# Output products in two halves of K, the first behind the last scores

## What is computed

```python
# first block: sliding-window heads (columns 0:512), differential heads (512:1024)
x = x + jnp.concatenate([out_a, out_b], axis=-1) @ w_out[l]
x = x + cross_attention(rms_norm(x, g_cross[l]), rms_norm(mem, g_mem[l]), w_cq[l], w_ckv[l], w_co[l])
x = x + jnp.square(jax.nn.relu(rms_norm(x, g_mlp[l]) @ w_up[l])) @ w_down[l]
# second block, two layers (mod = silu(c) @ ada_w + ada_b gives shifts, scales, gates)
x = x + 0.5 * g1[:, None] * swiglu(h, ff_w13[l, 0], ff_w2[l, 0])
y = hybrid_conv_mla(...)   # layer 0: concatenate([y_conv, y_att]) @ w_out
y = nsa_attention(...)     # layer 1: three gated branches, 16 heads, @ w_out
x = x + g2[:, None] * y
x = x + 0.5 * g3[:, None] * swiglu(h, ff_w13[l, 1], ff_w2[l, 1])
# the convolution of the hybrid mixer, 512 channels, 3 taps
y_conv = gate_b * short_conv(gate_c * u, conv_w)
```

## Time and profile before

| what | value |
|---|---|
| three runs, median | 1638.56 us (1635.45 to 1639.36) |
| the profiled execution | 1635.71 us |
| its span, first to last instruction | 1633.8 us |
| PE busy | 1480.9 us, 91% |
| DVE busy | 1096.8 us, 67% |
| ACT busy | 687.9 us, 42% |
| mean granted clock of TensorE | 0.948 of full speed |
| one low part of a unit, L780 | 2272 ns, 221 of them |
| one high part of a unit, L771 | 1895 ns, 221 of them |
| one term of the modulation, L1524 | 749 ns, 108 of them |

### The profile page before, as it was taken

How to read it: one execution, slowest core, us unless ns; L and a number is a source line. 1 busy time by engine, 2 the same in 40 slices (tenths; PEclk the granted TensorE clock), 3 DMA queues, 4 the chain that set the end, 5 groups by cost and what they waited for, 6 DMA issues and landing times.

```text
span 1633.8 us, 18297 instructions
## 1 busy us (share of the span) xinstructions
PE 1480.9 (91%) x7116; PEld 1225.1 (75%) x7116; DVE 1096.8 (67%) x1450; ACT 687.9 (42%) x917; POOL 56.6 (3%) x109
## 2 busy tenths in 40 slices
PE   4988688899997999989789999899998899799996
PEld 3776577788876888878768888688886767688885
DVE  4687664767666676675676667777668578675544
ACT  4445343344443443445434434344333656344342
POOL 4000000000001000010000000000000000000000
PEclk9999799899998999989789999899998899899999
DMA  8652242577763778746148778487784620455651
GB/s 285 230 205 78 70 150 77 186 266 236 279 232 125 262 234 281 235 162 192 52 155 282 257 263 282 137 285 257 258 260 163 200 78 1 154 194 185 201 180 64
DMA packets 188811, 314.24 MB, mean 192 GB/s; under 512 B 6912, under 2 KB 100407, under 8 KB 188727
## 3 DMA queue, kind: packets, MB, share of 16 engines
q1 hardware_dynamic: 148224, 231.82, 43.6%
q10 hardware_dynamic: 38678, 76.69, 13.0%
q0 software_dynamic: 1824, 4.57, 0.9%
HBM read 311.99 MB, written 1.07 MB: 192 GB/s over the span
## 4 chain that ended last, share of the span: by engine, by line
PE 80%; DVE 10%; ACT 5%; issue 2%; POOL 1%; DMA 1%; DVEq 0%; ACTq 0%; SPq 0%
PE ps L818 23%; PE ps L820 23%; PE ps L819 23%; PE ps L1090 2%; PE ps L827 2%; PE ps L847 2%; ACT whi L771 2%; PE ps L941 2%; PE ps L927 2%; PE ps L1045 1%; DVE wlo L780 1%; DVE rmax L1641 1%; DMA raw<-in_w_in 1%; POOL rstd L1931 1%; DVE x L1499 1%
## 5 line engine op out<-in xcount | busy, mean ns | idle before, releaser
L780 DVE TENSOR_TENSOR wlo<-raw,whi 128x2048 fp32r<-128x2048 f32 (+1 forms) x221 | 502.1, 2272 | 241.4 <-ACT whi L771 240.0
L818 PE MATMUL ps<-whi,aT 128*128 128x512 f32 (+1 forms) x1216 | 488.7, 402 | 3.7 <-ACT z L1223 3.7
L771 ACT ACTIVATE whi<-raw 128x2048 fp32r<-128x2048 f32 (+1 forms) x221 | 418.7, 1895 | 146.7 <-PE ps L820 112.1
L820 PE MATMUL ps<-wlo,aT 128*128 128x512 f32 (+1 forms) x1216 | 476.6, 392 | 0.0
L819 PE MATMUL ps<-whi,aTl 128*128 128x512 f32 (+1 forms) x1216 | 476.5, 392 | 0.0
L818 PEld LDWEIGHTS ps<-whi,aT 128*128 128x128 f32 x1216 | 234.1, 192 | 47.6 <-issue 4.1
L820 PEld LDWEIGHTS ps<-wlo,aT 128*128 128x128 f32 x1216 | 232.7, 191 | 48.6
L819 PEld LDWEIGHTS ps<-whi,aTl 128*128 128x128 f32 x1216 | 233.7, 192 | 43.6
L818 PE MATMUL ps<-whi,hT 128*128 128x512 f32 (+1 forms) x524 | 203.6, 390 | 9.1 <-DVE hTl L1576 7.7
L820 PE MATMUL ps<-wlo,hT 128*128 128x512 f32 (+1 forms) x524 | 200.6, 385 | 0.0
L819 PE MATMUL ps<-whi,hTl 128*128 128x512 f32 (+1 forms) x524 | 200.3, 384 | 0.0
(11 more groups left out here) (229 smaller groups left out, 1318.2 us busy)
## 6 DMA issues: line engine op xcount, KB each, us to landing
raw<-in_ff_w SPq DMA_DIRECT2D x176, 512.0 KB, 4.9
raw<-in_ff_w SPq DMA_DIRECT2D x44, 1024.0 KB, 5.2
qT<-in_ada_w ACTq DMA_DIRECT2D x36, 1024.0 KB, 6.4
pT<-in_ada_w ACTq DMA_DIRECT2D x36, 1024.0 KB, 7.6
raw<-in_w_up SPq DMA_DIRECT2D x16, 1024.0 KB, 5.7
raw<-in_w_down SPq DMA_DIRECT2D x16, 1024.0 KB, 5.1
raw<-in_w_in SPq DMA_DIRECT2D x9, 1024.0 KB, 7.4
raw<-in_w_ckv SPq DMA_DIRECT2D x8, 1024.0 KB, 5.8
```

The source lines that it names most:

```text
L771: act.activation(whi[:, slot, 0:m], raw[:, slot, 0:m], ACT.Copy).then_inc(w_hi, 1)
L780: dve.tensor_tensor(wlo[:, slot, 0:m], raw[:, slot, 0:m], whi[:, slot, 0:m].bitcast(F32), ALU.subtract).then_inc(w_lo, 1)
L818: pe.matmul(out_ap, hi, w, start=start, stop=False)
L820: return pe.matmul(out_ap, hi, wl, start=False, stop=stop)
```

## The change

Each of the four output products is cut in two halves of K. The first half (chunks 0 to 3) is issued inside the attention, by `out_first`, once for each column half, into the four banks that the last groups' scores have left; what it reads is turned earlier, by an `o_T` nested in an earlier step. Where it stands: in the first attention the turn at step 7 and the two parts at steps 8 and 9 (the first of them between the last transposes of probabilities and the last values); in the cross attention at 4 and, both, 5; in the hybrid one both at 5 (chunks 0 to 3 are the convolution's); in the third at 14, 20 and 21. The second half (`out_rest`) takes the two token tiles in turn and the two column halves in each. The groups of the cross and the third attention are reordered so that the first heads are done first. The taps of the convolution are taken from the attention and put behind the turn of the keys in the hybrid input product, in groups of four with one wait; its last product and its split stand behind that product, ahead of the attention. Modulation slots: two for an output product instead of four, a block starting every four or five slots from w_co on. A semaphore of its own (acc_done) counts finished sums.

```diff
+    def out_begin(self, w, gate=None):
+
+        wv = w.rearrange("(k p) n -> p k n", p=P)
+        last = self.groups[-1]["g"]
+        return dict(w=wv, gate=gate, banks=[2 * ((last + 1 + nb) % 2) for nb in range(2)],
+                    taken=[last + nb for nb in range(2)])
+
+    def out_unit(self, o, k0, nb):
+
+        return self.unit(lambda j: o["w"][:, k0:k0 + 4, 512 * nb:512 * nb + 512], 4, 512)
+
+    def out_first(self, o, nb):
+
+        u = self.out_unit(o, 0, nb)
+        self.mark_w(u)
+        self.stage("out_first", u=u, nb=nb, bank=o["banks"][nb], taken=o["taken"][nb], left=self.left[0:4])
+
+    def out_rest(self, o):
+
+        us = [self.out_unit(o, 4, nb) for nb in range(2)]
+        acc0 = self.acc_done
+        self.acc_done += 4
+        for nb in range(2):
+            self.used[us[nb]] = ("acc", acc0 + 3 + nb)
+        ev = [self.ada_unit() for nb in range(2)]
+        self.x_ready += NT
+        self.x_event = ("x", self.x_ready)
...
-    def o_turn(self, c0, c1, ready):
-        r = self.rounds((c1 - c0) // 2, "AD")
-        for c in range(KC):
-            self.left[c] = ("T", r[(c - c0) // 2]) if c >= c0 else ("conv", 1)
-        self.stage("o_T", chunk0=c0, rounds=r, ready=ready, fill=self.groups[-1]["fill"])
+    def o_turn(self, c0, ready, n=None):
+        r = self.rounds(2, "AD")
+        for c in range(c0, c0 + 4):
+            self.left[c] = ("T", r[(c - c0) // 2])
+        self.stage("o_T", chunk0=c0, rounds=r, ready=ready, n=n)
...
-        if self.ada_todo and self.ada_room >= 7 and (latest is None or latest["age"] >= self.ada_every[self.ada_n % 2]):
+        if self.ada_todo and self.ada_room >= 6 and (latest is None or latest["age"] >= self.ada_every[self.ada_n % 2]):
...
-    p.stage("attend", groups=attention_groups(p, "first"), which="first", turned=list(p.keys_turned), side=None)
+    out = []
+
+    def attend(which, turned, w, gate, nest):
+        groups = attention_groups(p, which)
+        out[:] = [dict(p.out_begin(w, gate), half=groups[len(groups) // 2 - 1])]
+        p.stage("attend", which=which, turned=turned, groups=groups, nest=attention_turns(p, groups, nest))
+
+    def first_half(n=None):
+        return lambda: p.o_turn(0, "U" if n is None else "nsa", out[0]["half"]["fill"] if n is None else n)
+
+    def early(nb):
+        return lambda: p.out_first(out[0], nb)
+
+    attend("first", list(p.keys_turned), A["w_out"][0], None, {7: first_half(), 8: early(0), 9: early(1)})
     p.stage("diff_norm", fill=p.groups[-1]["fill"])
-    p.o_turn(0, 8, "diff")
-    p.ada_until(8)
-    p.linear(A["w_out"][0], D, D, "x", "w_out")
+    p.o_turn(4, "diff")
+    p.ada_until(6)
+    p.out_rest(out[0])
     p.norm("x", D, ("prm", G_CROSS), eps=1e-5)
     p.linear(A["w_cq"][0], D, D, "z", "w_cq", flush=3)
     p.turned("qk_cross", 8, ["A", "D"] * 4)
-    p.stage("attend", groups=attention_groups(p, "cross"), which="cross", turned=list(p.keys_turned), side=None)
-    p.o_turn(0, 8, "U")
-    p.ada_until(73)
-    p.linear(A["w_co"][0], D, D, "x", "w_co")
+    def both():
+        early(0)()
+        early(1)()
+
+    attend("cross", list(p.keys_turned), A["w_co"][0], None, {4: first_half(), 5: both})
+    p.o_turn(4, "U", p.groups[-1]["fill"])
+    p.ada_every = (4, 5)
+    p.ada_until(71)
+    p.out_rest(out[0])
     p.norm("x", D, ("prm", G_MLP), eps=1e-5)
     p.mlp("relu2", A["w_up"][0], A["w_down"][0], N1, HB1, None, "mlp")
     p.stage("scale_x", n=p.norms, need=p.x_event, turn=len(p.T.who), eps=1e-5)
@@ -393,19 +443,22 @@
                 p.turned("q_mla", 4, ["A", "D"] * 2)
                 turned.extend(p.keys_turned)
 
...
-            def turn_k():
+            def turn_k_taps():
                 p.turned("k_mla", 4, ["A", "D"] * 2)
                 turned.extend(p.keys_turned)
+                p.stage("conv_taps", after=p.last_fill)
+
+            def conv_last():
+                p.stage("conv", after=p.last_fill)
+                p.left[0:4] = [("conv", 1)] * 4
 
             p.linear(A["hy_w_in_2"][0], D, 1952, "z", "hy_in", flush=3,
                      blocks=[(1536, 416, "z")] + [(c0, 512, "conv") for c0 in (0, 512, 1024)],
-                     inner={1: latent_stats, 2: latent_norms, 3: ups, 4: pack, 5: turn_q, 6: turn_k})
-            p.stage("attend", groups=attention_groups(p, "mla"), which="mla", turned=turned, side=p.last_fill)
-            p.stage("conv")
-            p.o_turn(4, 8, "U")
-            p.ada_every = (4, 5)
-            p.ada_until(76)
-            p.linear(A["hy_w_out_2"][0], D, D, "x", "hy_out", gate=(p.n_gates, 1.0))
+                     inner={1: latent_stats, 2: latent_norms, 3: ups, 4: pack, 5: turn_q, 6: turn_k_taps, 7: conv_last})
+            attend("mla", turned, A["hy_w_out_2"][0], (p.n_gates, 1.0), {5: both})
+            p.o_turn(4, "U", p.groups[-1]["fill"])
+            p.ada_until(74)
+            p.out_rest(out[0])
         else:
             turned, r_cmp = [], []
 
@@ -446,10 +499,10 @@
             p.linear(A["nsa_w_in_2"][0], D, 1840, "z", "nsa_in", flush=5,
...
+            attend("nsa", turned, A["nsa_w_out_2"][0], (p.n_gates, 1.0), {14: first_half(6), 20: early(0), 21: early(1)})
+            p.o_turn(4, "nsa", 12)
+            p.ada_until(35)
+            p.out_rest(out[0])
...
-        for br in (0, 1):
-            spec += [dict(kind="nsa", br=br, t=t, h0=h, nh=4) for t in range(NT) for h in (0, 4, 8, 12)]
-        spec += [dict(kind="cmp", t=t, h0=h, nh=8) for t in range(NT) for h in (0, 8)]
+        for half in (0, 8):
+            for br in (0, 1):
+                spec += [dict(kind="nsa", br=br, t=t, h0=half + h, nh=4) for t in range(NT) for h in (0, 4)]
+            spec += [dict(kind="cmp", t=t, h0=half, nh=8) for t in range(NT)]
...
+            def out_part(u, bank, tt, k0, left, start, stop):
+
+                use(lambda j: u)
+                wv = whi[:, u % RING, :].rearrange("p (a b) -> p a b", b=512)
+                wl = wlo[:, u % RING, :].rearrange("p (a b) -> p a b", b=512)
+                for k in range(4):
+                    if left:
+                        wait_left(left, k)
+                    last = three(ACC[:, bank + tt, :], aT[:, k0 + k, tt * P:(tt + 1) * P],
+                                 aTl[:, k0 + k, tt * P:(tt + 1) * P], wv[:, k], wl[:, k], start and k == 0, stop and k == 3)
+                return last
+
+            def out_first(st):
+                pe.wait_ge(s_taken, st["taken"])
+                for tt in range(NT):
+                    last = out_part(st["u"], st["bank"], tt, 0, st if tt == 0 else None, True, False)
+                last.then_inc(w_used, 1)
+
+            def out_rest(st):
+                for tt in range(NT):
+                    for nb in range(2):
+                        out_part(st["us"][nb], st["banks"][nb], tt, 4, st if tt == nb == 0 else None,
+                                 False, True).then_inc(acc_done, 1)
+                for ev in st["ev"]:
+                    for what, m in ev:
+                        if what == "ada_out":
+                            ada_out(m)
 
             def cmp_hid(st):
                 for kv, (u, t) in enumerate(zip(st["units"], st["rounds"])):
...
+            def out_first(st):
+                split_hi(act, lambda j: st["u"] + LEAD)
+
+            def out_rest(st):
+                for u, ev in zip(st["us"], st["ev"]):
+                    split_hi(act, lambda j: u + LEAD)
+                    for what, m in ev:
+                        if what == "ada_in":
+                            ada_load(m)
 
...
+            def out_first(st):
+                if st["nb"] == 0:
+                    split_lo(dve, lambda j: st["u"] + LEAD)
+
+            def out_rest(st):
+                us = st["us"]
+                split_lo(dve, lambda j: us[1])
+                split_lo(dve, lambda j: us[0] + LEAD)
+                terms(st["ev"][0])
+                k = 0
+                for tt in range(NT):
+                    for nb in range(2):
+                        dve.wait_ge(acc_done, st["acc0"] + k + 1)
+                        add_to_x(ACC[:, st["banks"][nb] + tt, :], tt, nb * 512, 512, k, st["gate"], None, nb == 1)
+                        k += 1
+                split_lo(dve, lambda j: us[1] + LEAD)
+                terms(st["ev"][1])
+
+            def terms(ev):
+                for what, m in ev:
...
+            def conv_taps(st):
+                wait_emptied(dve, U, lambda j: st["after"] - 1)
+                wait_emptied(dve, U, lambda j: st["after"])
+
+                def each(f):
+                    for k in range(4):
+                        n = step(f(k, zcf[:, k, :], tmp[:, k // 2, (k % 2) * S:(k % 2 + 1) * S],
+                                   [prm[:, CONV_W + 4 * t + k:CONV_W + 4 * t + k + 1] for t in range(3)]))
+                    dve.wait_ge(v_done, n)
+
+                each(lambda k, u, t, w: dve.tensor_tensor(t, zcf[:, 4 + k, :], u, ALU.mult))
```

(11 more changed lines are left out.)

85 lines of the change are left out of this document (41 added, 44 removed).

## The result

The change makes the kernel slower. Five runs after have a median of 1651.33 us (1646.51 to 1653.55), five of before on the same occasion 1635.45 us; the ratio is 1.0087, 95% interval 1.0061 to 1.0112. The forecast was 1631.2 us, with 1642 as the upper end of its range. One thing about the ratio matters further down: in the other experiments the kernel before has medians of 1639 to 1640 us over 95 runs, so the five beside this kernel lie some 4 us low.

A forecast was written before the change was run, and what follows sets the result against it. TensorE was taken as the bound, busy 1480.9 of 1633.8 us, with only idle time to win. Gains of 10.8 less 1.6 (tails) and 1.8 (modulation) gave 7.4 us: 1638.56 to 1631.2 us, range 1623 to 1642.

The forecast's parts named there:

- B: Cross attention to the end of its output product: the early first half fills idle time, a gain of 1.5 us.
- N: Third attention to its output product's end: 5.1 us less, net 2.6 after the group order and the nested turn.
- the tails: Output products into the next norms: a split between adds and squares costs 1.6 us in all.
- A: First attention to its output product's end: the early half fills the differential norm's gap, a gain of 4.2 us.
- Rival 3: Norms behind output products: the split costs the four tails 12.4 us instead of 1.6; kernel 1644 us; chance 0.14.
- rival 2: Nested turns in A and N hide wholly, tails cost nothing: gain 15.9 us, kernel 1622.7 us; chance 0.12.
- D: Hybrid attention to its output product's end: taps moved out, product ends at 832.3 us, a gain of 2.5 us.
- rival 1: Low clock through D's attention: total gain 0.9 us, kernel 1637.7 us; chance 0.29 with its special form.
- the order of the groups: Third attention: the new order costs about 1.0 us, from summing each step's longest engine part.
- The nested turn: Third attention: the first half's turn inside the stream costs 1.5 us, bounds 0 and 3.7.
- the modulation: Third block's input product: four last terms in one slot where two stood lengthen TensorE's wait, +1.5 us.

The follow-up runs named there:

- snake: Kernel after with the third attention's groups reordered for fewer changes of width, halves and nested turn kept; ratio to before 1.0036.
- late_unit: Kernel before with the last modulation block of the third input product started one unit later; ratio to before 0.9982.
- gate_late: Kernel after with the third input product's gate store tied to a modulation output one unit later; ratio to before 1.0035.
- phase: Kernel after with modulation units started every four units, instead of four and five, from the hybrid output product on; ratio to before 1.0009.
- best1: Kernel after with the third attention's narrow groups in the old order and modulation every four units from the hybrid output product on; 1629.93 us, ratio to before 0.9948.
- best3: Kernel after with the third attention's order of snake, modulation every four units, and the taps back inside the hybrid attention; ratio to before 0.9949.
- gate_extra: Kernel before with one added store of 4-byte elements, issued at 1262.85 us in the third input product; ratio to before 1.0002.

## Why the prediction was wrong

**Right: B, the end of N, the tails; A with luck.** The last turn in A came at 179.8 (forecast 180.0), the last values at 187.1 (189.0), the product's end at 212.04, which is 216.61 less 4.57 (212.1). That end is two errors that cancel: the norm was done at 196.3 (198.2), and the second half behind it took 15.8 us, where 13.9 were counted (13.1 and half a chance of the low clock, 0.8) and B and N took 13.3; the clock was low for its first 7 us. B's first scores moved from 254.91 to 251.97 and its product's end from 299.7 to 295.2, a gain of 1.5 to 1.6 (1.5). In N, from the last turn to the product's end, 4.4 us (5.1). From the product's last matmul to the next product: 9.2 us in A (9.5 forecast), 10.3 in N (10.6). Rival 3, the split between adds and squares, is ruled out by these, and rival 2 by D and N. Of what A and B gained, 1.1 us went in the cross attention's input product, where the prediction charged 0.3; why, no run shows.

**Wrong by rival 1: D.** The prediction gave the product's end as 832.3 with the clock high and 838.8 with it low. In the kernel after it is 835.11 - 2.49 = 832.6 with first scores 4.76 us earlier, so 837.4 on that scale: 2.6 us lost, not 2.5 won. On that scale the first maximum came at 787.7 (788.0 forecast); from it to the end of the last values were 23.6 us (20.4), and from there to the product's end 26.1 (24.0). The step that failed is the 5.1 us taken off for the low clock of the last two groups, and with it the high clock at the start of the first parts. (The terms that the prediction lists for the 20.4 add up to 20.2.) It failed as a bet on the clock and not as a sum: in snake, where the same stage kept the high clock, the product's end is at 834.41 - 2.50 = 831.9, 150.0 us behind the first scores, or 830.9 on that scale, against 832.3 forecast. The rule set beside it was that of "TensorE: Matmul & The Clock Gate" of the Trainium skill (Part 1), that activity releases the throttle. In the kernel after the clock did come back to 2.4 GHz at about 790 us and was lost again at 797, and from there the close transposes and narrow values stayed at 1.2 GHz to the end of the attention, as in the row of the old kernel; in one of seven profiled executions of this stage they didn't.

**Wrong: the order of the groups, 1.0 us priced, 11.8 measured.** The step was "I summed, for each step of the loop, the longest of the three engines' parts". That sum leaves out every wait of one engine for another within a step. The traces show the waits and on whom, ScalarE's copy of the transposed probabilities; how they arise I can only argue: a step's turn needs ScalarE's exponentials of the group before, and the values need its copy of the transposes, so where a group of one width follows one of another, TensorE finishes its short part and waits for the long part of the others, and later the other way round. The old order has 1.1 us of such waits, the new one 8.1, and 5.4 us more idle time in all; the rest, 6.4 us, is the clock behind them, which a sum by steps doesn't hold at all. The nested turn, priced at 1.5 with bounds of 0 and 3.7, makes no difference that can be told: 80.18 us with it and 80.03 without, in one execution each.

**Wrong: the modulation, 1.5 us priced, 9.0 measured.** The step was "the last four terms then fall in one slot where two stood". That shift of four terms costs nothing by itself (late_unit). What I didn't follow is everything else that hangs on the schedule: the gate's store goes out with the sum that the plan names, and a shift of one output by three units moved it by 21 us, into the loads. 6.3 of the 9.0 us are the store's (gate_late, from one execution of each); a modulation load held in ScalarE's queue for 4.3 us is the likely rest, as the wait of 4.27 us stays in gate_late and shrinks to 1.0 in phase and in best1, but no run moved that load alone. The prediction counted the moved terms, and neither the loads that they need nor the store behind them.

**The sum.** With A +4.5, B +1.6, the ends as found, D -2.6, N +4.4 - 11.9 = -7.5, the third input product -9.0, and some +0.5 net of the tails, the other input products and the feed-forward stretches, the balance is the 12.5 us of the two spans. The forecast named a lengthened feed-forward stretch as what would refute it; single ones did move (the first by -2.7, the second by +3.3 us, by the start of their successors at 508.8 and 713.6 us against 515.7 and 717.2), but in sum they cancel.

## What to carry to other kernels

Before moving a piece of a schedule, list what is released by it, small stores included, and look in the trace at what would be in flight at the new time; a transfer of 4 KB in single elements can hold up 2 MB of loads. Reordering the groups of a software pipeline isn't free even if every engine's total stays the same: look for each place where a group of one width follows one of another and TensorE would be ready before its input (seven such waits of 0.9 to 1.6 us here), and then reckon with the clock behind them. A count of the changes isn't a price: with five in place of four, snake and best3 wait 4.4 and 4.9 us longer. And before a stage's time is put down to an edit, look at the granted clock and at the same stage in kernels that leave it alone: here one stage took 58.6 and 65.1 us with the same instructions. Split a product for early issue only as far as idle time stands behind the last head (8.08 us in A, 1.51 in N), and pay nothing upstream for it.

## What the hardware showed that was not expected

A store of 4 KB in 1024 pieces of 4 bytes takes 9.0 to 14.1 us from issue to landing. Beginning about 3 us behind its issue, the core's other DMAs move mostly under 90 GB/s together instead of 300 to 400, wherever loads were looked at beside it (before, after, gate_late, gate_extra, phase). "DMA: Bandwidth & Descriptors" of the Trainium skill says (Specifications) that below 512 B a transfer isn't at line rate and is done as read-modify-write, and (Queues, rings and completion order) that each DMA engine goes round its queues packet by packet, many descriptors to a packet. The traces fit that: the slow packets of one queue take the others' turns. That this is the mechanism wasn't tested.

One stage can run at two clocks with the same instructions. The third attention in one order took 72.0 us at a granted clock of 0.98 (best3) and 77.0 at 0.88 (snake), with 64.3 and 70.5 us of TensorE busy. The hybrid stage took 58.6 us at 0.90 (snake) and 65.1 at 0.77 (after), with 41.7 and 48.7 us of TensorE busy for the same 218 matmuls. Whether the other stages of the kernel or the single execution decides it isn't shown.
